# Expert weights in transfers of 3 MB into a ring of four places, and two split experts instead of three

## The reference

```python
def swiglu(h, w1, w3, w2):
    return (jax.nn.silu(h @ w1) * (h @ w3)) @ w2

def moe_ffn(h, router_w, w1, w3, w2):
    logits = (h @ router_w).astype(jnp.float32)
    top_vals, top_idx = lax.top_k(logits, TOP_K)
    top_w = jax.nn.softmax(top_vals, axis=-1)
    gate = jnp.sum(jax.nn.one_hot(top_idx, N_EXPERTS, dtype=jnp.float32) * top_w[..., None], axis=-2)
    out = jnp.zeros_like(h)
    for e in range(N_EXPERTS):
        out = out + gate[..., e:e + 1].astype(h.dtype) * swiglu(h, w1[e], w3[e], w2[e])
    return out
```

## Time and profile before

| | us |
|---|---|
| median of 3 runs | 2193.1 |
| lowest and highest | 2192.41, 2194.68 |
| the profiled execution | 2195.61 |
| its span, from the first to the last instruction | 2193.8 |
| PE busy in the span | 2101.6 (96%) |
| DVE busy | 1351.1 (62%) |
| ACT busy | 1010.5 (46%) |

### The profile page before, as it was taken

One profiled execution on the slowest core, in us unless ns is written; L12 is line 12 of the kernel. 1 busy time (PEld: TensorE's weight loads), 2 busy tenths in 40 slices (PEclk: granted clock), 3 DMA queues, 4 the chain that ended last, 5 costly groups with the idle time before them and its releaser, 6 DMA issues.

```text
span 2193.8 us, 38945 instructions
## 1 busy us (share of the span) xinstructions
PE 2101.6 (96%) x15459; PEld 1783.2 (81%) x15459; DVE 1351.1 (62%) x2457; ACT 1010.5 (46%) x1759; POOL 125.0 (6%) x115
## 2 busy tenths in 40 slices
PE   8999989999999999999999999998999999999998
PEld 7988888998988898889999898888556866866774
DVE  5565667566668676878665775775116825834942
ACT  5545544545544453456444453443005614623731
POOL 0100000000000032030000032030000000000000
PEclk9999999999999999999999999998999999999999
DMA  6443324544336453355555453358999999999996
GB/s 201 145 137 97 97 97 146 155 132 141 116 129 157 137 165 107 113 172 174 175 197 163 122 154 116 98 171 354 406 421 421 421 410 420 416 370 420 419 363 269
DMA packets 257820, 489.50 MB, mean 223 GB/s; under 512 B 35256, under 2 KB 208216, under 8 KB 223720
## 3 DMA queue, kind: packets, MB, share of 16 engines
q1 hardware_dynamic: 252112, 484.39, 61.1%
q0 software_dynamic: 656, 1.80, 0.2%
q10 hardware_dynamic: 4872, 0.81, 0.2%
HBM read 485.91 MB, written 1.05 MB: 222 GB/s over the span
## 4 chain that ended last, share of the span: by engine, by line
PE 45%; DVE 5%; ACT 2%; DMA 1%; issue 1%; POOL 1%; DVEq 0%; POOLq 0%; SPq 0%; ACTq 0%
PE bank L862 8%; PE bank L869 8%; PE bank L1356 7%; PE bank L660 5%; PE bank L903 4%; PE bank L896 4%; PE bank L629 3%; DVE memr L2417 1%; PE bank L823 1%; DMA mem_tail<-in_moe 1%; PE bank L878 1%; POOL mem_high L1789 1%; PE bank L923 1%; PE bank L925 0%; PE bank L540 0%
## 5 line engine op out<-in xcount | busy, mean ns | idle before, releaser
L1356 PE MATMUL bank<-memr 128*128 128x256 f32 (+3 forms) x7056 | 898.3, 287 | 29.2 <-DVE memr L2417 9.7
L1356 PEld LDWEIGHTS bank<-memr 128*128 128x128 f32 (+2 forms) x7056 | 857.3, 186 | 59.5 <-issue 16.3
L2417 DVE TENSOR_TENSOR memr<-mem_low,memr 128x1024 fp32r<-128x1024 f32 (+3 forms) x328 | 400.4, 1239 | 64.3 <-ACT memr L1864 63.6
L1864 ACT CAST memr<-mem_low 128x1024 fp32r<-128x1024 f32 (+3 forms) x328 | 333.3, 1032 | 113.5 <-PE bank L1356 109.0
L1053 ACT ACTIVATE mem_high<-bank 128x128 f32<-128x128 f32 (+1 forms) x88 | 28.0, 318 | 301.0 <-PE bank L869 253.9
L1252 DVE SCALAR_TENSOR_TENSOR mem_high<-mem_high,bank 128x128 f32<-128x128 f32 (+1 forms) x88 | 29.5, 335 | 212.2 <-ACT mem_high L1053 212.2
L862 PE MATMUL bank<-memr 128*128 128x512 f32 x400 | 131.5, 396 | 3.0 <-DVE memr_tail L1200 3.0
L660 PE MATMUL bank<-memr 128*128 128x256 f32 x960 | 115.6, 281 | 3.1 <-DVE memr L2436 3.1
L660 PEld LDWEIGHTS bank<-memr 128*128 128x128 f32 x960 | 114.3, 189 | 3.5 <-issue 3.5
L869 PE MATMUL bank<-mem_tail,mem_low 128*64 128x256 f32 x896 | 105.0, 388 | 0.6 <-DVE mem_low L1211 0.6
L1200 DVE TENSOR_TENSOR memr_tail<-mem_tail,memr 128x2048 fp32r<-128x2048 f32 x39 | 88.7, 2288 | 25.2 <-ACT memr L1020 24.8
(11 more groups left out here) (367 smaller groups left out, 3024.6 us busy)
## 6 DMA issues: line engine op xcount, KB each, us to landing
mem_tail<-in_moe SPq DMA_DIRECT2D x132, 1024.0 KB, 11.6
mem_ring<-in_moe SPq DMA_DIRECT2D x128, 1024.0 KB, 12.6
mem_low<-in_w_in SPq DMA_DIRECT2D x112, 1024.0 KB, 5.1
mem_tail<-in_ffn_w SPq DMA_DIRECT2D x18, 1024.0 KB, 8.4
mem_low<-in_w_out SPq DMA_DIRECT2D x16, 1024.0 KB, 5.5
mem_low<-in_w_branch SPq DMA_DIRECT2D x12, 1024.0 KB, 5.0
mem_high<-in_ffn_w SPq DMA_DIRECT2D x12, 1024.0 KB, 7.9
mem_low<-in_w_branch SPq DMA_DIRECT2D x16, 512.0 KB, 3.6
```

What stands on the lines that cost most here:

```text
L1356: ins = pe.matmul(out(bank), lhsT, rhs, start=((k, i) == order[0] and not half), stop=((k, i) == order[-1]), skip_group_check=half is not ...
L1864: cp(high, raw).then_inc(*sig("w_high", i))
L2417: st(V.tensor_tensor(low, raw, high, ALU.subtract), sig("w_split", i))
```

## The change

- `HEAVY` is 2 instead of 3, so ranks 1 and 2 alone have 128 places; rank 3 gets 64 and is light. `TURN` changes from [0, 4, 1, 5, 2, 6, 3, 7] to [0, 3, 1, 4, 5, 2, 6, 7]: the third and the sixth expert in order are split.
- The weights lie in HBM as one row of 24 KB (6144 numbers) per partition and chunk: 4096 numbers of up weights and 2048 of down weights, the latter rolled by two chunks, so that a row holds what one step of PE uses. There are 90 loads (`LOADS`) instead of 264. Loads 0 and 1 have only up weights, 88 and 89 only down weights. A load of 3 MB is one DMA if its place is contiguous, two (rows of 16 KB and 8 KB) if the place is the fourth of the ring, or if the load is one of the first two of an expert, when its down weights belong to the expert before.
- There are five places at first and four (`SLOTS`) in the ring, each of 3 MB. Four loads are allowed ahead of the stage (two of 2 MB, two of 3 MB), the fifth when the routing is chosen. Load k waits for the last tile of load k-4 (k-5 for the first four), which is the down tile of step k-4.
- `raw_loaded` waits for the whole load. Light and split arithmetic are unchanged.

The core of the diff:

```diff
-HEAVY = 3
+HEAVY = 2
-TURN = [0, 4, 1, 5, 2, 6, 3, 7]
+TURN = [0, 3, 1, 4, 5, 2, 6, 7]
-RAW = 12
+SLOTS = 4
-FIRST = RAW + HI
+FIRST = SLOTS + 1
+LOADS = UPS + 2
...
+        def load_of(n):
+            g, j = TILE_ORDER[n]
+            return g if j < 2 else g + 2
+        def place_of(k):
+            return k if k < FIRST else (k - FIRST) % SLOTS
+        def transfers(k):
+            if k >= UPS or k < 2:
+                return 1
+            return 1 if k % HALF >= 2 and whole_place[place_of(k)] is not None else 2
+        def last_tile(k):
+            return down_tile(k - 2) if k >= 2 else up_tile(k, 1)
...
-                for n in range(TILES):
-                    g, j = TILE_ORDER[n]
-                    i, c = divmod(g, HALF)
+                for k in range(LOADS):
+                    i, c = divmod(k, HALF)
...
-                        sp.wait_ge(*tile_done(p, n - (FIRST if n < FIRST + RAW else RAW)))
-                    src = a["moe"][bass.DynSlice(expert[i], 1), c, j].rearrange("o p f -> (o p) f") if i else a["moe"][0, c, j]
-                    sp.dma_start(raw[slot_of(n)], src).then_inc(raw_loaded(p, n)[0], 16)
+                        sp.wait_ge(*tile_done(p, last_tile(k - (FIRST if k < FIRST + SLOTS else SLOTS))))
+                    place, (ups_, down_) = place_of(k), load_place[place_of(k)][0]
+                    if transfers(k) == 1 and 2 <= k < UPS:
+                        sp.dma_start(whole_place[place], weights(expert, i, c, 0, 6144)).then_inc(family(f"m_raw{place}"), 16)
+                    else:
+                        if k < UPS:
+                            sp.dma_start(ups_, weights(expert, i, c, 0, 4096)).then_inc(family(f"m_raw{place}"), 16)
+                        if k >= 2:
+                            before = (k - 2) // HALF
+                            sp.dma_start(down_, weights(expert, before, c, 4096, 6144)).then_inc(family(f"m_raw{place}"), 16)
...
-                        pe.sem_inc(family("m_done"), RAW)
+                        pe.sem_inc(family("m_done"), SLOTS)
...
-    moe = np.empty((EXPERTS, HALF, 3, P, 2048), np.float32)
+    moe = np.empty((EXPERTS, HALF, P, 6144), np.float32)
```

More of the change, by code:

```diff
@@ L315, in build @@
         top[0] = upper
-        raw, raw_r = map(list, zip(*[carve_both(2048) for _ in range(6)]))
+        load_place, whole_place = [], []
+        for _ in range(2):
+            both = carve_both(6144)
+            whole_place.append(both[0])
+            load_place.append([(v[:, 0:4096], v[:, 4096:6144]) for v in both])
         top[0] = mark
-        for i in range(5):
-            raw.append(mem_ring[:, 2048 * i:2048 * (i + 1)])
-            raw_r.append(carve_both(2048)[1])
+        both = mem_ring[:, 0:6144], carve_both(6144)[1]
+        load_place.append([(v[:, 0:4096], v[:, 4096:6144]) for v in both])
+        ups_f, ups_r = mem_ring[:, 6144:10240], carve_both(4096)[1]
         htok = [carve(D)]
@@ L323, in build @@
         top[0] = -(-(after_z + ccols["decay"][0] - c_first) // 8) * 8
[L324 to L325 removed]
+        down_f = mem_ring[:, top[0] - at_ring:top[0] - at_ring + 2048]
+        load_place.append([(ups_f, down_f), (ups_r, carve_both(2048)[1])])
         assert top[0] <= after_z + c_all - c_first
+        assert len(load_place) == SLOTS
         top[0] = 0
[L328 to L330 removed]
+        wide_hi, wide_hi_r = carve_both(6144)
+        load_place.append([(wide_hi[:, 0:4096], wide_hi[:, 4096:6144])] * 2)
+        whole_place += [mem_ring[:, 0:6144], None, wide_hi]
+        hi_r = [wide_hi_r[:, 2048 * i:2048 * (i + 1)] for i in range(3)]
         hi_f = [v.bitcast(F32) for v in hi_r]
@@ L758, in heavy_before, with raw_tile, raw_tile_r @@
             return sum(heavy(k) for k in range(i))
-        def slot_of(n):
-            return n if n < FIRST else (n - FIRST) % RAW
-        def raw_loaded(p, n):
-            k = slot_of(n)
-            if k >= RAW:
-                last = max(range(k - RAW, len(chunks), NSLOT))
-                s, before = at(f"w_loaded{k - RAW}", last)
-                return s, p * 16 + before + 16
-            loads = len(range(k, TILES - FIRST, RAW)) + 1
-            return family(f"m_raw{k}"), p * 16 * loads + 16 * (1 if n < FIRST else (n - FIRST) // RAW + 2)
+        def load_of(n):
[3 more added lines that the diff above has]
+            return k if k < FIRST else (k - FIRST) % SLOTS
+        def raw_tile(n, form=0):
+            j = TILE_ORDER[n][1]
+            ups_, down_ = load_place[place_of(load_of(n))][form]
+            return down_ if j == 2 else ups_[:, 2048 * j:2048 * (j + 1)]
+        def raw_tile_r(n):
+            return raw_tile(n, 1)
+        def transfers(k):
+            if k >= UPS or k < 2:
+                return 1
+            return 1 if k % HALF >= 2 and whole_place[place_of(k)] is not None else 2
+        def raw_loaded(p, n):
+            k, s = load_of(n), place_of(load_of(n))
+            of_place = [q for q in range(LOADS) if place_of(q) == s]
+            each, so_far = sum(map(transfers, of_place)), sum(transfers(q) for q in of_place if q <= k)
+            return family(f"m_raw{s}"), 16 * (p * each + so_far)
+        def last_tile(k):
+            return down_tile(k - 2) if k >= 2 else up_tile(k, 1)
         def split_done(p, n):
@@ L977, in moe_sync, with weights @@
         def moe_sync(sp):
+            def weights(expert, i, c, lo, hi):
+                if i == 0:
+                    return a["moe"][0, c][:, lo:hi]
+                return a["moe"][bass.DynSlice(expert[i], 1), c][:, :, lo:hi].rearrange("o p f -> (o p) f")
             def body(p, learn):
                 expert = {0: 0}
-                for n in range(TILES):
-                    g, j = TILE_ORDER[n]
-                    i, c = divmod(g, HALF)
-                    if i not in expert:
+                for k in range(LOADS):
+                    i, c = divmod(k, HALF)
+                    if k < UPS and i not in expert:
                         r = TURN[i]
```

35 lines of the change are left out of this document (15 added, 20 removed).

## The result

The kernel after takes **2200.44 us** (median of 7 runs, 2197.38 to 2204.76), the kernel before 2192.41 us in the 7 runs beside it (2189.8 to 2194.76). The ratio is **1.0039, with a 95% interval from 1.0028 to 1.0051**: slower by 0.4%, some 8 us. The forecast was 2190.0 us with 2183 to 2201 as its range, so the time lies just inside the range, on the side that was not forecast. The profiled execution took 2197.38 us with a span of 2195.5 us.

What follows compares the result with a forecast made beforehand. PE was taken as the bound before, DMA a close second; afterwards weight loads, with PE's 35 us saving becoming about 32 us of waits. The chain gave a 2190.7 us span, 3.1 below before; off median 2193.1, 2190.0 us, range 2183 to 2201.

Steps and rivals of the forecast that it cites:

- chain: Expert stage, from one restart of the load queue to the next, through two split experts to the end: span 2190.7 us.
- Coarser places: Ring of weight places: a 3 MB place frees at step end; no loss in pure waiting, 2.3 us latency per restart.
- steps 1, 5 and 6: Queue restarts at loads 5, 37 and 70: each lands 9.7 us after the work that frees its place.
- step 4: First split expert: eleven split steps and one light take 106.9 us; loads 23 to 36 catch up meanwhile, filling the ring.
- the twelve steps from entry to release: Both split experts: eleven split steps and the first light one, until a place is freed, 106.9 us each time.
- The granted clock stays 1.00: Expert stage: a sign expected in the profile, that TensorE's clock stays at the 2.4 GHz level despite its waits for weights.
- The fallen clock: Rival: TensorE's clock falls in waits, counting at two split entries and the tail; 9 us, 2199 us; 10 in 100.
- The stream: Expert-stage weight loads following one another without a stop: 7.39 us per load, with 0.15 us saved by longer rows.
- the 3.1 that I had taken off: Whole kernel: forecast span 2190.7 us is 3.1 us below the span before; this difference was taken from the median 2193.1.
- The rival that the rows bring nothing: Weight loads: each stays at 7.54 us despite longer rows, 8.3 us more, 2198.3 us; 17 in 100.
- the one with the 13952-byte row: Rival for weight loads: at that packet row's rate, 8.5 us per load, 61 us more, 2251 us; 2 in 100.
- PE stays the bound: Rival for the expert stage: all saved PE work is kept, 2156 us, needing loads under about 6.5 us; 3 in 100.

Runs made afterwards that it cites:

- e5: Kernel after plus 20 small matmuls with overwritten results ahead of each split expert's first up matmul, where PE waits; 2198.23 us, 1.0018 to the kernel before.
- e10: Kernel before's 1 MiB tile ring with two split experts in the new order, 13 tiles of lead, places freed at step end; 2192.95 us, 0.9997 to the kernel before.
- e3: Kernel after with each load issued as three DMAs with 8 KB rows into the same place, under the same wait; 2203.37 us, 1.0043 to the kernel before.

## Why the prediction was wrong

Its chain was the right one, and can be held against the trace interval by interval. The ends of work are those of the matmul groups, the landings those of the loads.

| step | forecast us | after us |
|---|---|---|
| 1: step 0's up matmuls end at | 1532.9 | 1527.1 |
| 1: load 5 lands after | 9.7 | 11.1 |
| 2: loads 6 to 22 | 125.6 | 125.3 |
| 3: landed tile to split matmul | 4.3 | 4.4 |
| 4: twelve steps | 106.9 | 108.7 |
| 5: load 37 lands after | 9.7 | 10.9 |
| 5: loads 38 to 55 | 133.0 | 133.8 |
| 6: entry | 4.3 | 4.3 |
| 6: twelve steps | 106.9 | 109.5 |
| 6: load 70 lands after | 9.7 | 11.5 |
| 6: loads 71 to 87 | 125.6 | 126.4 |
| 7: tail | 22.05 | 22.4 |

**Two terms were mis-sized, each by 4.4 us.** The first is the restart of the queue, in "Coarser places" and in steps 1, 5 and 6: 2.3 us of latency plus a load at full pace, 9.7 us, where it took 10.9 to 11.5, three times. The step that failed stands in step 4: "Meanwhile loads 23 to 36 ... catch up, and the ring is full". They had not all landed. In the split expert of the kernel after, a place comes free once per step, every 8.5 us or so, and a load issued then needs 10 us: so load 36 was still on its way for 2.1 us when load 37 was issued, and load 69 for 2.2 us at load 70. Into an empty queue a load took 10.3 us there (load 35) and 11.0 at the stage's start (load 5). Latency and overlap with the load before don't add up to the measured times: behind loads 36 and 69 the next one landed 8.6 and 9.2 us later, not 7.4. Why, and why load 5 took 11.0, is open.

The second is the twelve steps from entry to release, 108.7 and 109.5 us against 106.9. "The granted clock stays 1.00" was wrong for the one wait that is long, and right for the many that are short. The fallen clock was on the list as a rival with 10 in 100 and 9 us; it came in the two entries and not in the tail. e5 shows 2.8 us of the 4.4 as the clock's. The rest, which shows in e5 with the clock at 1.00, is mostly the first entry, where the loads behind the first one come late. The stream and the tail add 1.8 us more, and all together 10.6 us.

**The start hid half of it.** In this execution step 0 ended 5.8 us early. 3.1 us of that lie ahead of the stage, where nothing was changed (its last mixer product ended at 1507.3 instead of 1510.4 us); most of the rest is the half clock at the stage's start, which lasted less long (10.2 instead of 17.1 us; 5.01 instead of 6.54 us for the first 32 matmuls). Hence a span of 2195.5, only 4.8 us over the forecast; with the start of the earlier trace rows it would be 2201. By differences the account closes better: 2193.1, plus the 10.6, minus the 3.1 that I had taken off, is 2200.6, and the median is 2200.44. That it closes to 0.2 us is luck, since the executions of the kernel after alone lie up to 7.4 us apart.

**The stream was right.** Loads came every 7.41 us on average (52 loads in 385.5 us), 7.39 were forecast; rows of 24 KB in fewer DMAs save 0.11 us against 0.15. The rival that the rows bring nothing fell, and so did the one with the 13952-byte row. The Trainium skill's figure ("DMA: Bandwidth & Descriptors", Why small descriptors are slow), from which an estimate of 0.06 us per load was worked out, is below the 0.11 that the runs show, in which the number of DMAs changes too. That PE stays the bound fell too; 31.6 us of saved work became 27.7 us of waits in light steps, besides the entries. The waits are where they were forecast, in the second light expert of each pair, none after a split one, and the routing fitted in one pass.

**The clock's rule.** The prediction held that by the Trainium skill ("TensorE: Matmul & The Clock Gate", HAM oscillation) the fallen clock would be the forecast. It left out that the wait in that page's example is longer than the matmuls between two waits. Here 23 light steps of 5.6 us ended in waits of up to 1.7 us and ran at 1.00, and only the waits of 4.7 and 4.8 us took the clock down. The trace does not contradict the page.

**What the prediction did not ask** is what the coarse ring costs against a fine one under the same new work. It weighed places only where the ring stands full, and called them "no loss" in a waiting stretch; the chain holds the loss in its steps 1, 4 and 5 without naming it. Priced so, from e10 and e3, it is 26 us against the 6 us of the rows in the traces, of which the ratios show 0.9, uncertain by 4.

## What to carry over

When transfers become the bound, a ring is worth what its queue keeps moving: count the time from the use of a piece to the issue of the next one into its place, and from a landing to the first use that waits for more than it needs. Larger transfers bring the fixed part of their packets and DMAs, here 0.11 us in 7.4; if they must be large, release and wait for their parts separately. A forecast from one profiled execution should be made by differences between intervals, since what lies ahead of the change and the clock at the stage's start moved its end by 5.8 us here.

## What the hardware showed

- A load of 3 MB issued into an empty queue landed after 10.3 us in one case and 11.0 in another; issued 2.1 and 2.2 us before the load ahead of it had landed, after 10.7 and 11.3. The steady pace was 7.41 us. As three DMAs (e3) the first MiB landed 4.9 to 5.0 us after its issue; the second came 2.5 us later in one load and 3.9 in another, the third 2.5 us after that in both.
- Rows of 8 KB ran at 420 GB/s in a full stretch, rows of 24 KB, in fewer DMAs, at 427 to 428.
- Waits of TensorE of up to 1.7 us behind 5.6 us of work left the granted clock at 1.00. Waits of 4.7 and 4.8 us took it to 0.50 for 6.8 us in the kernel after; in e3, waits of 5.1 and 5.0 us did so for half as long. Small matmuls in that wait kept it at 1.00, and cost nothing that a trace shows.
